# Filler products ahead of the last bands, and four out-projection products moved between attention units, in a two-block transformer kernel

## The reference, cut to what matters

```python
for l in range(DEPTH):                       # DEPTH = 2
    h = rms_norm(x, g_norm_mix[l]) * (1 + sc1) + sh1
    z = h @ w_in[l]
    # mixed = concat(A: 6 attention heads over the top 64 keys, 384 columns,
    #                B: 6 heads of a gated recurrence, 384 columns,
    #                C: gated MLP over chunks of 128 tokens, 256 columns)
    x = x + g1 * (mixed @ w_out[l])
    # layer 0: dense gated MLP; layer 1: eight experts, two for each token
```

## Time and profile before

| what | value |
|---|---|
| median of 3 runs | 2324.07 us (2318.11 to 2326.15) |
| the profiled execution | 2321.18 us |
| its span in the profile | 2319.3 us |
| PE busy | 2232.3 us, 96% |
| DVE, ACT busy | 912.4 us (39%), 391.3 us (17%) |
| chain that ended last | PE 86%, DMA 6%, DVE 4% |
| mean granted PE clock | 0.98 of full |

### The profile page before, as it was taken

One profiled execution on the slowest core, in us unless ns is written; L12 is line 12 of the kernel. 1 busy time (PEld: TensorE's weight loads), 2 busy tenths in 40 slices (PEclk: granted clock), 3 DMA queues, 4 the chain that ended last, 5 costly groups with the idle time before them and its releaser, 6 DMA issues.

```text
span 2319.3 us, 36138 instructions
## 1 busy us (share of the span) xinstructions
PE 2232.3 (96%) x15385; PEld 1565.7 (68%) x15386; DVE 912.4 (39%) x2181; ACT 391.3 (17%) x971; POOL 49.1 (2%) x81
## 2 busy tenths in 40 slices
PE   7999999999999999998999999989999999999999
PEld 5867998877754444433444444357679998769999
DVE  3674887548320000000000010024667734547764
ACT  3232110222220000000000000014421002531100
POOL 1010000001000000000000000000000000000000
PEclk8998999999899999999999999999999999999999
DMA  9562678934079999999988999993325463333541
GB/s 354 189 219 73 199 233 327 377 114 146 32 265 374 376 410 411 409 411 409 401 306 343 409 410 409 412 356 115 109 75 180 168 188 109 135 110 110 177 152 54
DMA packets 242165, 582.99 MB, mean 251 GB/s; under 512 B 24251, under 2 KB 108739, under 8 KB 229717
## 3 DMA queue, kind: packets, MB, share of 16 engines
q1 hardware_dynamic: 241428, 580.52, 67.6%
q0 software_dynamic: 576, 0.13, 0.0%
HBM read 579.58 MB, written 1.05 MB: 250 GB/s over the span
## 4 chain that ended last, share of the span: by engine, by line
PE 86%; DMA 6%; DVE 4%; issue 1%; SPq 1%; ACT 1%; POOL 0%; DVEq 0%; POOLq 0%
PE wrk L2672 13%; PE acc L1024 8%; PE acc L3481 5%; PE acc L2732 5%; PE acc L3515 5%; PE wrk L2657 4%; PE wrk L3481 4%; PE wrk L3515 4%; DMA ring<-in_moe_w_gate_dram 4%; PE acc L1027 3%; PE acc L1805 3%; PE wrk L2679 3%; PE acc L1825 3%; PE wrk L1805 3%; PE acc L1101 2%; PE acc L2715 2%
## 5 line engine op out<-in xcount | busy, mean ns | idle before, releaser
L2672 PE MATMUL wrk<-ring,hT 128*64 128x512 f32 (+1 forms) x1792 | 352.0, 546 | 12.6 <-DMA ring<-in_moe_w_gate_dram 6.0
L2916 DVE TENSOR_TENSOR scratch<-scratch,wrk 128x512 f32<-128x512 f32 (+4 forms) x32 | 24.6, 768 | 793.7 <-PE wrk L2672 585.5
L2672 PEld LDWEIGHTS wrk<-ring,hT 128*64 128x64 f32 x1792 | 127.7, 138 | 213.8 <-issue 185.7
L1024 PE MATMUL acc<-hT,ring 128*128 128x256 f32 x1024 | 231.3, 381 | 0.0
L1024 PEld LDWEIGHTS acc<-hT,ring 128*128 128x128 f32 x1024 | 192.0, 190 | 27.9 <-issue 2.0
L2732 PE MATMUL acc<-ring,scratch 128*64 128x512 f32 x784 | 177.3, 597 | 8.6 <-DMA ring<-in_moe_w_down_dram 7.8
L3560 DVE TENSOR_TENSOR ring<-ring 128x512 f32<-128x512 f32 (+1 forms) x192 | 155.2, 864 | 1.1
L2732 PEld LDWEIGHTS acc<-ring,scratch 128*64 128x64 f32 x784 | 53.9, 137 | 113.1 <-issue 101.6
L3515 PE MATMUL acc<-scratch,ring 128*128 128x128 f32 x1024 | 117.6, 276 | 0.0
L3515 PEld LDWEIGHTS acc<-scratch,ring 128*128 128x128 f32 x1024 | 116.0, 192 | 0.0
L2851 ACT ACTIVATE scratch<-wrk 128x512 f32<-128x512 f32 (+4 forms) x32 | 21.2, 661 | 481.9 <-PE wrk L2704 481.9
(11 more groups left out here) (485 smaller groups left out, 2952.4 us busy)
## 6 DMA issues: line engine op xcount, KB each, us to landing
ring<-in_moe_w_gate_dram SPq DMA_DIRECT2D x56, 2048.0 KB, 19.1
ring<-in_moe_w_up_dram SPq DMA_DIRECT2D x56, 2048.0 KB, 21.1
ring<-in_moe_w_down_dram SPq DMA_DIRECT2D x56, 2048.0 KB, 22.5
ring<-in_w_ada_dram SPq DMA_DIRECT2D x24, 2048.0 KB, 17.1
ring<-in_w_up_dram SPq DMA_DIRECT2D x32, 1024.0 KB, 7.1
ring<-in_w_down_dram SPq DMA_DIRECT2D x32, 1024.0 KB, 6.2
ring<-in_w_out_dram SPq DMA_DIRECT2D x8, 2048.0 KB, 8.8
ring<-in_w_in_dram SPq DMA_DIRECT2D x10, 1536.0 KB, 11.5
```

What stands on the lines that cost most here:

```text
L1024: mm = pe.matmul(acc[p0:p0 + m, bank, 0:S], cols(k), hT[:, k, :], start=(k == 0), stop=(k == KD - 1))
L2672: mm = pe.matmul(flat_wrk[h * HD:h * HD + HD, lo:lo + n2], hT[:, k, 0:HD], w[:, at_, h * n2:(h + 1) * n2], start=(k == 0), stop=(k == KD - ...
```

## The change

It has three parts. At the head of band j, for j from 13 on in layer 0 and from 11 on in layer 1, PE runs one filler product (8 in all: 3 and 5), behind a wait for "c out". In layer 1, `outproj_first_pe` for output row 0 by slots 6 and 7 runs behind `inter_pe` beside unit 3, and the same for row 1 beside unit 4 (the first also behind a wait for "c out"). In layer 1, the former pass over rows 0 and 1 with five slots becomes `outproj_more_pe` with slots 0 to 2. The number of products of the out-projection stays as it was. `items` is made ahead of `att_pe`.

```diff
+        BUSY_FROM = (13, 11)
...
             for j in range(C):
+                if j >= BUSY_FROM[l]:
+                    pe.wait_ge(dve_done, at("dve", "c out", l, 1))
+                    keep_busy_pe(pe, 1)
                 band_pe(pe, l, j)
...
                 else:
                     inter_pe(pe, l, u - 3)
+                    if l and u < 5:
+                        if u == 3:
+                            pe.wait_ge(dve_done, at("dve", "c out", l, 1))
+                        outproj_first_pe(pe, items[0], 0, range(u - 3, u - 2), ATTENDED[3:])
...
+            items = out_items("out1", l)
             att_pe(pe, tag, branches1(l), beside)
-            items = out_items("out1", l)
             pe.wait_ge(dve_done, at("dve", "o", l))
             outproj_first_pe(pe, items[1], 1, range(0, 2), ATTENDED[3:])
             head_sums_pe(pe, l)
             pe.wait_ge(dve_done, at("dve", "head out", ("1", l), 5))
-            outproj_first_pe(pe, items[0], 0, range(2), ATTENDED)
+            if l:
+                outproj_more_pe(pe, items[0], 0, range(2), ATTENDED[:3])
+            else:
+                outproj_first_pe(pe, items[0], 0, range(2), ATTENDED)
```

## The result

The changed kernel is slower by a little: 2327.43 us median of 22 runs (2323.15 to 2332.20) against 2323.32 of 22 runs of the kernel before; ratio 1.0016, 95% interval 1.0010 to 1.0022, which is 3.7 us (2.3 to 5.1). That lies inside the forecast range (2316 to 2328) and inside the 0.3% that was called the same, but on the other side of no change than the forecast (2322.4). It is the time of the rival "the clock comes back late" (2327.8).

The account below looks back on a forecast made before the run. PE's chain and its granted clock were taken to bound the kernel. Fillers +0.86, layer 1 -1.0, layer 0 -0.4, move +0.3 and units -1.4 gave -1.6 us: 2322.4 us on a median of 2324.07, range 2316 to 2328.

Parts of the forecast that it names:

- the clock comes back late: Rival, chance 0.10: layer 1's later units end after the clock's return, out-projection passes run slow; +3.7 us, 2327.8 us.
- What bounds, and whether a gain lasts: Layer 1's chain is DVE's in the bands, mostly PE's behind; its gain or loss reaches the end one for one.
- The fillers' cost: Bands: 0.43 us on the path at layer 1's band 11 and layer 0's band 13, others 0; sum +0.86 us.
- The fillers' gain in layer 1: Bands to kv: the clock's fall at 569.6 us is held off or moved back; between 0 and 1.58, taken -1.0 us.
- the 0.4 us: Layer 0, kv and ada piece: fillers gain part of a 1.5 us bound by a higher clock; taken -0.4 us.
- 1.50 of 3.40 us: Layer 0: PE's busy time in the stretch just ahead of the clock's fall, said to have made it fall.
- The moved products: Layer 1, out-projection calls beside units 3 and 4: 0 at full clock, up to +0.88 us if slow; taken +0.3.
- The clock in the units: Layer 1 units and item 1: wide moved products hold the clock up; between 0 and 2.8, taken -1.4 us.
- PE's idle time and the clock: Layer 1, 590 to 593.4 us: PE was never idle, and the clock still fell.

Follow-up runs that it names:

- e1_fillers: The eight fillers alone added to the kernel before, out-projection unchanged; 2323.72 us against 2324.61, ratio 1.0000.
- e10_fill12: Fillers in layer 1 alone, from band 12, added to the kernel before, no moved calls; 2322.62 us against 2324.18, ratio 1.0000.
- e3_ahead: Kernel before with both moved calls ahead of the first `inter_pe` and the later pass shortened, no fillers; 2328.65 us against 2324.61, ratio 1.0018.
- a_again: The changed kernel itself measured once more, against the kernel before; 2326.48 us against 2324.18, ratio 1.0014.
- e4_idle: Kernel before with the moved calls ahead of kv of units 1 and 2, later pass shortened, no fillers; 2329.55 us against 2324.61, ratio 1.0020.
- e9_place: Changed kernel, all fillers kept, with the moved calls ahead of kv of units 1 and 2 instead; 2324.07 us, ratio 0.9997 to the kernel before.
- e2_moved: The two calls behind `inter_pe` alone, no fillers, against the kernel before; 2326.33 us against 2324.61, ratio 1.0009.
- c_shift5: Kernel before with five filler products ahead of layer 1's last out-projection products; 2328.91 us against 2324.07, ratio 1.0012.

## Why the prediction was wrong

- **What bounds, and whether a gain lasts**: right. DVE in the bands, PE in the units and behind; in the pair of profiles with before and the changed kernel the 1.2 us of layer 1 and what the norm adds are still there at the end.
- **The fillers' cost**: right. 0.43 us on the path in each layer, ahead of bands 13 and 11, and nothing ahead of the others (in layer 0 the stretch from the last projection to `inter_pe` grew by 0.44 us).
- **The fillers' gain in layer 1**: right that the fall comes later. In all eight profiles with fillers the first fall came 8 to 24 us behind the last projection, in the six without 3 to 5 us. The size isn't a thing to count on. After gained 1.4 us net of the 0.43, so 1.9 gross, with 1.0 forecast and 1.58 as the bound, which had left out the transposes of unit 1 (0.35 us). But e1_fillers lost 3.1 us in the same stretch and e10_fill12 1.4, and the times of the kernels with fillers alone are at 1.0000. In e1_fillers the later falls met the scores (1.68 us for unit 0) and two kv groups (2.03 and 1.99 us). In layer 0 the 0.4 us weren't there: kv of unit 0 took 1.76 us and the ada piece 2.75, as before. That the stretch of 1.50 of 3.40 us "made the clock fall" there is not shown; the rows have only a fall behind it.
- **The moved products**: "at the full clock the move itself is worth 0" holds nearly in e3_ahead (2.03 us against 1.77, the clock at 1.00 from 590.9 us, 0.6 us behind their start). The +0.3 for the slow case was too small: both calls ran at the low clock, in both profiles of the changed kernel, at 0.50 us a record against 0.221, so 4.00 us in place of 1.77. With the 1.72 that the shortened pass gives back that is +2.3 in after, where +0.3 was forecast: 2.0 us off.
- **The clock in the units, the step that failed**: "Between 0 and 2.8 I take half, 1.4". It supposes, as the +0.3 does, that the 256-column products behind the first `inter_pe` keep the clock at 1.00 from there. In both profiles of the changed kernel the clock had fallen before the first call (at 590.9 in after, 592.1 in a_again), and no such gain came. From the first `inter_pe` to L1116 the sum for after is +4.00 (calls) - 1.72 (the shortened pass, 2.70 against 4.42) + 0.53 (item 1) + 0.16 and - 0.35 (transposes) = +2.6, and the profile has 40.2 - 37.6 = 2.6. Forecast were +0.3 - 1.4 = -1.1: 2.0 us of the difference are the price of the calls, 1.7 the units, which became 0.3 us longer in place of 1.4 shorter. The clock did come back behind the calls, at 601.2 us (in all three profiles with calls behind `inter_pe` it is up for a while between 600.6 and 605.8, in the other eleven it is low throughout from 597.7 to 605.6), but onto `inter_pe`, which takes 3.4 us at either clock (3.42 at 0.50, 3.41 at 1.00 in after), and it fell again before the work that would have used it.
- **The rivals**: the late return, with 0.10, came nearest. Its time, 2327.8, was met to 0.4 us, and that is luck: its +3.7 was to arise in the two mixers, which are 1.7 us longer in after's profile, and the rest of the 6.4 us there came behind them. Its parts came in part: two slow calls instead of one (+2.2 against +0.88), item 1's pass 3.46 us (3.54 forecast), the next twelve not doubled in after but so in e4_idle (5.47). Its ground, that nothing had raised the clock in the units, doesn't hold: before has 0.50 to 583.2 us and 1.00 from 583.3. What it lacked is the norm and what is behind it: the shift meets other falls there.
- **PE's idle time and the clock**: right that the clock fell with PE never idle. In before it fell at 593.5 behind 3.40 of 3.40 us of busy PE, and it stayed at 0.50 in after from 591 to 601 us with PE busy for 10.00 of 10.00 us, and in e4_idle for 22.92 of 23.70. The moved calls bought nothing, but what makes the clock fall or come back, no run shows.

What is shown: with the fillers in, the place of the two calls costs 3.9 us (1 to 7), which covers the 3.7 (e9_place against a_again). By the profiles they cost because each holds PE at the low clock for 2.0 us with nothing to hide behind. That this place is worse than the others without the fillers isn't shown. What is only likely: how the rest of a difference between two executions divides over norm, experts and second block, since it differs in every profile and intervals of 2 us can't price it. Open is why e4_idle is 4.6 us slower (2.3 to 7) than before while the same calls with fillers (e9_place) are not, and why e3_ahead is 4.2 us slower (1.9 to 6.5). e4_idle's one profile has the late return, but it is of one of its two fastest executions.

## What to carry to other kernels

Work moved on an engine's own path is worth the difference of its price in the two places: look up the granted clock there (a call of four records held PE for 2.00 us at 0.50 in after, for 0.97 at 1.00 in e2_moved), and look for a wait that ends with another engine (here ACT, ahead of kv), where part of it hides: in e4_idle's profile the stretch with both calls, one of them at the lower clock, grew by 0.7 us, and in e9_place the loss of the changed kernel was gone. Then measure: e4_idle as a whole was slow all the same. A gain or loss by the clock that one profile shows is one draw: price an edit by its range over several profiles, and ask what the higher clock would land on, since the 60 16-column products took 3.4 us at 0.50 as at 1.00. A shift of 2.2 us also changed how later stages met the falls, by 1.4 us in one norm and 1.7 us between the second block's out-projections (c_shift5).

## What the runs showed of the hardware

- With PE busy for 22.92 of 23.70 us the clock stayed at 0.50, through transposes, values, 16-column and 2-column products and two passes of 256-column ones (e4_idle, 594.3 to 618 us). It was back as the second of these passes ended.
- A group of 60 records of 16 columns took 3.42 us at 0.50 (after, 594.37) and 3.40 at 1.00 (e3_ahead, 592.31). In after the clock was at 1.00 from 601.2 to 604.5 us, just under such a group, which took 3.41 us.
- Four records of the out-projection as a group on their own took 2.00 us at the low clock (0.50 each), 12 took 5.33 in e4_idle's chain (0.44 each) against 2.70 at the full clock (0.23 each).
- The norm of layer 1 was 4.9 us long in the six of fourteen profiles in which its eight filler records took 1.73 us (in before the clock was at 1.00 from 636 to 650 us), and 6.3 to 6.6 us in the others, where they took 2.64 to 3.37 us (in after it was at 0.50 from 642.2 to 645.4). In the second block eight such records took 2.42 us in before, at 0.50 from 1928.2 to 1931.4, and 3.41 in after, at 0.50 from 1932.4 to 1939.1, first before and then after:

```profile
1930.22 2.42 PE acc L898 x8
```

```profile
1935.24 3.41 PE acc L898 x8
```
